# A hybrid decoder step on one core: block sums of the compressed cache taken on VectorE instead of in the accumulating gathers

## The reference, cut to what matters

```python
def block_means(rows):
    B, L = rows.shape[:2]
    nc = L // CMP_BLOCK                       # CMP_BLOCK = 32
    blk = rows[:, :nc * CMP_BLOCK].astype(jnp.float32).reshape((B, nc, CMP_BLOCK) + rows.shape[2:])
    return blk.mean(axis=2).astype(rows.dtype)

past_c = pool_c[page_table].reshape(B, PAST_LEN, 2, NSA_KV_HEADS, NSA_HD)
kc = jnp.concatenate([block_means(past_c).astype(kvc.dtype), block_means(kvc)], axis=1)
```

## Time and profile before

| | before |
|---|---|
| three runs, us | 2081.39, 2088.65, 2123.76 (median 2088.65) |
| the profiled execution's time, us | 2088.65 |
| its span, us | 2086.9 |
| mean granted TensorE clock | 0.931 |
| moved by DMA | 248.81 MB, mean 119 GB/s |

### The profile page before, as it was taken

How to read it: one execution, slowest core, us unless ns; L and a number is a source line. 1 busy time by engine, 2 the same in 40 slices (tenths; PEclk the granted TensorE clock), 3 DMA queues, 4 the chain that set the end, 5 groups by cost and what they waited for, 6 DMA issues and landing times.

```text
span 2086.9 us, 25824 instructions
## 1 busy us (share of the span) xinstructions
PE 1906.2 (91%) x9819; PEld 1313.0 (63%) x9819; DVE 639.6 (31%) x1498; ACT 588.6 (28%) x1251; POOL 425.2 (20%) x514
## 2 busy tenths in 40 slices
PE   4997895899988999997799998999799999999996
PEld 3886674677867765554466666774377777763332
DVE  3232232225000135543546561121233333330002
ACT  2232221222101135563465653003411111110103
POOL 2344234332000111113666630000000000000000
PEclk8998987998998759999999999999899999999998
DMA  7899979982631100002687877211322222211111
GB/s 180 194 214 234 210 180 216 228 196 88 195 85 48 33 10 1 1 1 66 201 278 254 274 227 226 81 61 61 86 61 61 61 78 64 61 61 51 61 38 45
DMA packets 201013, 248.81 MB, mean 119 GB/s; under 512 B 32201, under 2 KB 173850, under 8 KB 192538
## 3 DMA queue, kind: packets, MB, share of 16 engines
q1 hardware_dynamic: 176684, 134.16, 22.0%
q0 software_dynamic: 21248, 109.46, 21.5%
q10 hardware_dynamic: 2960, 3.54, 0.5%
HBM read 236.09 MB, written 19.29 MB: 122 GB/s over the span
## 4 chain that ended last, share of the span: by engine, by line
PE 58%; issue 17%; DMA 13%; DVE 4%; POOL 3%; ACT 3%; SPq 1%; ACTq 1%; POOLq 0%; DVEq 0%
DMA mem<-in_cache_cmp_kv,pidx 12%; PE ps L1505 11%; PE ps L1952 9%; PE ps L1516 5%; PE ps L1739 5%; PE ps L1897 3%; PE ps L1848 3%; PE ps L1826 3%; PE ps L1803 3%; PE ps L1537 2%; PE ps L1722 2%; PE ps L1751 2%; PE ps L1834 1%; PE ps L1587 1%; PE ps L1741 1%
## 5 line engine op out<-in xcount | busy, mean ns | idle before, releaser
L1505 PE MATMUL ps<-mem 128*128 128x288 f32 x1536 | 396.0, 421 | 1.6 <-DVE mem L1380 0.8
L1505 PEld LDWEIGHTS ps<-mem 128*128 128x128 f32 x1536 | 302.7, 198 | 87.6 <-DVE mem L1084 1.0
L1927 PE MATMUL ps<-mem 128*128 128x288 f32 x1408 | 349.4, 410 | 0.0
L1927 PEld LDWEIGHTS ps<-mem 128*128 128x128 f32 x1408 | 267.6, 191 | 72.5
L678 POOL DMA_INDIRECT mem<-in_cache_sel_kv,sidx x192 | 184.0, 958 | 294.1 <-PE ps L1686 194.3
L1952 PE MATMUL ps<-mem 128*128 128x512 f32 (+1 forms) x440 | 203.6, 608 | 0.0
L1952 PEld LDWEIGHTS ps<-mem 128*128 128x128 f32 (+1 forms) x440 | 72.0, 179 | 130.9 <-issue 130.8
L641 POOL DMA_INDIRECT mem<-in_cache_cmp_kv,pidx x56 | 90.2, 1610 | 238.1 <-DMA mem<-in_cache_cmp_kv,pidx 235.7
L708 POOL COPY mem<-mem 128x2 f32<-128x2 f32 x44 | 11.6, 264 | 610.6 <-ACT mem L994 610.6
L1739 PE MATMUL ps<-mem 64*128 64x128 f32 (+3 forms) x256 | 115.4, 537 | 2.1 <-ACT mem L876 2.1
L1516 PE MATMUL ps<-mem 128*128 128x256 f32 (+1 forms) x480 | 107.8, 385 | 0.0
(11 more groups left out here) (300 smaller groups left out, 2292.1 us busy)
## 6 DMA issues: line engine op xcount, KB each, us to landing
mem<-in_cache_sel_kv SPq DMA_DIRECT2D x320, 128.0 KB, 4.4
mem<-in_w_up SPq DMA_DIRECT2D x44, 512.0 KB, 5.1
mem<-in_w_in SPq DMA_DIRECT2D x32, 512.0 KB, 10.2
mem<-in_w_in SPq DMA_DIRECT2D x14, 1024.0 KB, 5.0
mem<-in_w_down SPq DMA_DIRECT2D x10, 1024.0 KB, 4.9
mem<-in_state_win_kv SPq DMA_DIRECT2D x16, 512.0 KB
out<-in_state_win_kv POOLq DMA_DIRECT2D x8, 1008.0 KB, 16.0
mem<-in_x_prompt SPq DMA_DIRECT2D x8, 512.0 KB, 6.5
```

The source lines that it names most:

```text
L1505: mm = t.matmul(ps[:, 2 * (u % 2) + a, 0:NHF], lhs(k), hT[:, k, a * NHF:(a + 1) * NHF], start=(k == 0), stop=(k == KD - 1))
L1927: mm = t.matmul(ps[:, 2 * (u % 2) + a, 0:NHF], lhs(k), hT[:, k, a * NHF:(a + 1) * NHF], start=(k == 0), stop=(k == KD - 1))
```

## The change

All 64 gathers become plain ones. They take the three slots of `cring` in turn (k % 3 for gather k), and a gather waits only until the slot's former content has been added up (`cg_used` of k - 2). DVE takes each slot with a `tensor_reduce` over its four positions (a view `p c r`: 512 results, groups of four numbers that lie 512 numbers apart), into `cmt[:, b, :]` for q = 0 and into the new buffer `cpart` for q = 1 to 7, and then adds `cpart` to `cmt`. These `rowsum` steps stand at three places of every iteration h < 8: two ahead of `states(h - 1)`, three between `prep2(h)` and `kq(h)`, three behind `kq(h)`. POOL issues three gathers before everything else, eight in head 0, and four and four at the two places of each later head. The old `block_sums` is gone.

```diff
@@ -169,6 +169,7 @@
 
         CROW = 4 * 2 * KV
         cring = [view(CROW, a_kvt + i * CROW) for i in range(3)]
+        cpart = view(2 * KV)
 
         at[0] = a_r
         qb, gb, eb, rb, fb, xb = [[view(N) for _ in range(2)] for _ in range(6)]
@@ -482,7 +483,6 @@
             bb, cc = divmod(kq - NVR, NPC + 1)
             return NC * bb + cc + 1
         NCST = 30
-        CG_STEP = 4
 
         WSEQ = [("wo", 0)] + [x for i in range(1, TT) for x in (("wo", i), ("tr", i - 1))] + [("tr", TT - 1)]
 
@@ -623,26 +623,20 @@
             assert done[0] == NCST, done[0]
 
             pool.wait_ge(idx_ok, 1)
-            ticks = [0]
+            gathers = [0]
 
             def gather(n):
                 for _ in range(n):
-                    k = ticks[0]
-                    for b in range(SB):
-                        q = k - CG_STEP * b
-                        if not 0 <= q < 8:
-                            continue
-                        if q == 0:
-                            wait(pool, cg_used, b - 2)
-                            pool.indirect_dma_start(cring[b % 3], None, cache_rows,
-                                                    bass.IndirectOffsetOnAxis(pidx[:, b, 0:1], 0)).then_inc(cg_in[b % 3], 16)
-                        else:
-                            pool.wait_ge(cg_in[b % 3], 16 * (8 * (b // 3) + q))
-                            pool.indirect_dma_start(cring[b % 3], None, cache_rows,
-                                                    bass.IndirectOffsetOnAxis(pidx[:, b, q:q + 1], 0),
-                                                    compute_op=ALU.add).then_inc(cg_in[b % 3], 16)
-                    ticks[0] += 1
-
+                    k = gathers[0]
+                    if k == SB * 8:
+                        return
+                    wait(pool, cg_used, k - 2)
+                    b, q = divmod(k, 8)
+                    pool.indirect_dma_start(cring[k % 3], None, cache_rows,
+                                            bass.IndirectOffsetOnAxis(pidx[:, b, q:q + 1], 0)).then_inc(cg_in[k % 3], 16)
+                    gathers[0] += 1
+
+            gather(3)
             for h in range(HH + 1):
                 if h < HH:
 
@@ -661,12 +655,12 @@
                     g.tensor_tensor(vms[0:S], vo[0:S, PT, :].unsqueeze(1).to_broadcast([S, SB, P]),
                                     cmask_s[:, :].unsqueeze(2).to_broadcast([S, SB, P]), ALU.mult).then_inc(vm_ok, 1)
                     if h < HH:
-                        gather(2)
+                        gather(4)
                     pool.wait_ge(st_ok, 5 * h)
                     pool.dma_start(hgo_p[0, 0, o, :, :], st[:, NCH, :]).then_inc(hgo_out, 16)
                     pool.dma_start(hgo_s[0, :, o, :, :].rearrange("b k v -> k b v"), s1s).then_inc(hgo_out, 16)
                 if h < HH:
-                    gather(5 - 2 * (h > 0))
+                    gather(8 - 4 * (h > 0))
             for b in range(SB):
                 pool.dma_start(win_s[0, b, 0:WIN - ST].rearrange("w h g d -> w (h g d)"),
                                win_kv[0, b, ST:WIN].rearrange("w h g d -> w (h g d)")).then_inc(win_out, 16)
@@ -810,7 +804,7 @@
                 if new:
                     h_sig(h, 0, qb)
                 else:
-                    act.wait_ge(cg_used, SB)
+                    act.wait_ge(cg_used, SB * 8)
                     kv_rows(U_KV)
                 if old:
                     h_ktok(h - 1)
@@ -1092,12 +1086,23 @@
             mark(v.memset(att, 0.0))
             mark(v.memset(att_s, 0.0))
 
-            def block_sums(b):
-
-                r = cring[b % 3]
-                dve.wait_ge(cg_in[b % 3], 16 * 8 * (b // 3 + 1))
-                link(v.tensor_tensor(r[:, 0:4 * KV], r[:, 0:4 * KV], r[:, 4 * KV:8 * KV], ALU.add))
-                v.tensor_tensor(cmt[:, b, :], r[:, 0:2 * KV], r[:, 2 * KV:4 * KV], ALU.add).then_inc(cg_used, 1)
+            sums = [0]
+
+            def rowsum(n):
+
+                for _ in range(n):
+                    k = sums[0]
+                    if k == SB * 8:
+                        return
+                    b, q = divmod(k, 8)
+                    dve.wait_ge(cg_in[k % 3], 16 * (k // 3 + 1))
+                    out = cmt[:, b, :] if q == 0 else cpart
+                    ins = v.tensor_reduce(out, cring[k % 3].rearrange("p (r c) -> p c r", r=4), AX.X, ALU.add)
+                    ins.then_inc(cg_used, 1)
+                    dve.wait_ge(cg_used, k + 1)
+                    if q:
+                        link(v.tensor_tensor(cmt[:, b, :], cmt[:, b, :], cpart, ALU.add))
+                    sums[0] += 1
 
             def prep2(h):
 
@@ -1170,22 +1175,21 @@
 
             for h in range(HH + 1):
                 new, old = h < HH, h > 0
-                if not new:
-                    block_sums(SB - 1)
                 if old:
                     silu(h - 1, 3, gb, 2 * h)
                 if new:
                     silu(h, 0, qb, 2 * h + 1)
                 if old:
                     masked(h - 1)
+                if new:
+                    rowsum(2)
                 if old:
                     states(h - 1)
                 if new:
                     prep2(h)
+                    rowsum(3)
                     kq(h)
-                for b in range(SB):
-                    if new and (CG_STEP * b + 7) // 5 + 1 == h:
-                        block_sums(b)
+                    rowsum(3)
                 if old:
                     head_out(h - 1)
```

## The result

| | kernel before | changed kernel |
|---|---|---|
| median of four runs beside each other | 2085.02 us (2080.42 to 2123.76) | 2156.22 us (2155.26 to 2161.16) |
| ratio | 1 | 1.0358, 95% interval 1.0335 to 1.0382 |

A forecast was written before the change was run, and what follows sets the result against it. PE's stalls for POOL's masked values, queued behind serial gathers, were taken as the bound; new DVE sums make the heads 8.8 + 7 x 61.3 = 437.9 us instead of 415.7, so 2088.65 + 22 = 2111 us, range 2025 to 2165.

The forecast's parts named there:

- The stalls at L658 go: Recurrence heads: all 52.5 us of PE's waits for POOL's masked values vanish; at most 73.4 us gained.
- DMA at the plain rate isn't the limit: Head stage: plain gathers move 295 GB/s, so a head's 11.6 MB take 39 us and supply does not limit.
- The reduce at 3.63 us: DVE row sums: a 2048-element reduce with jumps costs 1.70 ns an element plus 154 ns, as L1044 did.
- slower rival: DVE reduce: jumps of 2048 bytes cost twice the unit price, 4.41 us; 67.5 us a head, 2159 us total; chance 0.30.
- fast rival: DVE reduce: jumps are free, 2.28 us; loop 50.2 us a head, 2025 us total; chance 0.20.
- 61.3 us a head and 8.8 for the first: Head loop: 58.3 us with six sums before head_out plus 3.0 for PE's clock; first head waits 8.8 for a bank.
- the paragraph on new waits: Head stage: POOL waits for slot sums, delaying state stores, loads and masked values; costed at nothing.
- Behind the last head nothing changes: All stages after the recurrence heads keep their former time; no cost added.

The follow-up runs named there:

- nosum: Changed kernel with the row sums left out (eight-element copies in place of the reduces, means missing): 2110.53 us, ratio to before 0.9918.
- cont: Changed kernel with the reduce over four adjacent elements instead of strided ones (sums the wrong quadruples): 2038.77 us, ratio to before 0.9583.
- again2: Changed kernel unaltered, rerun and profiled on a further chip: 2157.86 us, ratio to before 1.0325; the profiled run took 2160.7 us.
- again: Changed kernel unaltered, for a second profile: 2163.02 and 2164.29 us in two runs, 2209.65 and 2214.01 in two; lower groups' ratio to before 1.0168.
- again3: Changed kernel unaltered, on a last chip; with again4 fourteen runs: eight at 2164.95 to 2178.72 us, six at 2203.32 to 2221.66.
- again4: Changed kernel unaltered once more, same chip as again3; with it fourteen runs: eight at 2164.95 to 2178.72 us, six at 2203.32 to 2221.66.
- fill_before: Kernel before with four dummy matmuls ahead of each of the prompt attention's first 64 units: 2137.87 to 2166.03 us, ratio to before 1.0277.

## Why the prediction was off, step by step

- **The stalls at L658 go.** Right: none is left among PE's waits.
- **DMA at the plain rate isn't the limit.** Right. Landings fell from 10.7 to 6.2 us, and nosum runs at 49.7 us a head with all the gathers in place, at 238 GB/s. (In the changed kernel itself the rate over 104 to 480 us is 190, below before's 210, since POOL waits 336.6 us for DVE.)
- **The reduce at 3.63 us.** It measured 3.68. L1044, the one small reduce with jumps, gave 1.70 ns an element; the new one has (3684 - 154) / 2048 = 1.72. Jumps of 2048 bytes cost what jumps of 32 do: the slower rival's doubled price has no ground here. The fast rival's 2.28 us is what cont measured with the jumps taken out. The Trainium skill's page "SBUF — State Buffer" (section "Door 1: The DMA port swizzle") has a penalty for each access that enters a new 16-byte line. These runs agree with it, 1.40 us for 2048 elements; none of them has a jump inside a line, which would test it. The skill's page "VectorE: DVE Perf Modes" (section "The perf-mode tier table") has tensor_reduce at 1x in every column, and its table has no column for jumps: adjacent elements ran at 1.04 ns each, those 2048 bytes apart at 1.72.
- **61.3 us a head and 8.8 for the first.** again2 starts its keys at 77.07, 147.19, 207.48, 268.35, 329.51, 390.79, 452.15 and 519.68. The first interval (70.1) has the wait of 9.1 in it, 61.0 without; the next five are 60.3 to 61.4. The last is 67.5, and this was not foreseen: one DVE instruction takes 7.08 us there instead of 0.82, with POOL's masked values running beside it (last section). The sum is 442.6 us, where 437.9 were forecast and before had 415.7: +27 instead of +22. Without those 6.3 us it would be 436.3. So the one step of the head stage that failed is in the paragraph on new waits, which cost POOL's masked values at nothing: it asked what PE pays when they come late, and not what DVE pays when they run beside it.
- **"Behind the last head nothing changes".** This is the step that failed. The prediction took every later stage from one profiled execution as if it were fixed, and with it the 72 us at half clock at the start of the prompt attention. That length is drawn anew in each execution. In the comparison that was measured it fell short on three of before's four runs and long on all four of the changed kernel's, which put 36 us on top of the change's own cost. The two runs beside the profiled one, 2081 and 2124, had it in plain sight: 42 us between runs of one kernel were a stage with more than one length, not scatter.
- **What the change costs, like against like.** Means of the groups of runs, us:

| chip of | stretch | before (runs) | changed kernel (runs) | difference |
|---|---|---|---|---|
| first comparison | long | 2123.8 (1) | 2157.2 (4) | 33 |
| again | short | 2128.0 (3) | 2163.7 (2) | 36 |
| again | long | 2161.5 (4) | 2211.8 (2) | 50 |
| again2 | long | 2123.9 (8) | 2158.1 (6) | 34 |
| again3, again4 | short | 2125.1 (1) | 2170.8 (8) | 46 |
| again3, again4 | long | 2171.2 (16) | 2212.1 (6) | 41 |

By stages it is 27 us from first to last keys. By the first scores of the prompt attention it is 30 to 35 us between profiles of one chip (746.7 of again2 against 715.1 of fill_before, which is before up to there; 747.0 and 747.8 against 713.3 on the last chip). What is left up to 50 us I can't place: the long stretches come in more than one length (271 and 284 us of the stage), and the sample attention came out between 6 us shorter (again4, 366.6 against 372.2) and 8 longer (again, 372.1 against 364.5) than in a profile of before on the same chip.

Of the 71 us, then, some 35 are the change's and some 36 the draw's. The direction of the forecast was right and so was its mechanism in the head stage; its own size was 22 for some 35, and of the 49 us between forecast and measurement 36 come from what it left out. That 2156.22 us lies inside the stated range of 2025 to 2165 is luck: the upper end was set by a reduce of 4.41 us, and the reduce took 3.68.

The better version comes from the same reading. The gain on gathers is real, and the price was the stride: with two adds over adjacent halves in place of the strided reduce, the sums take 2.6 us instead of 4.4 and nearly fit DVE's idle time. That kernel is 0.974 to 0.981 of before, like against like on two chips, and some 86 us under the changed one on the last chip (2079 to 2093 against 2165 to 2179).

## What to carry to other kernels

Before a forecast is made against one profiled execution, look at its granted clock stage by stage and at the distance of its runs: a stage at 0.50 in the profile and runs that lie 40 us apart say that the baseline has more than one length, and a difference must be taken like against like. When DMA work is moved to DVE, work out the order of DVE's queue up to the instruction that PE waits for, and price a reduce by its stride: here it was cheaper to add halves twice than to reduce over jumps once. Look as well at what POOL runs beside the new instructions of DVE: those here that read two tensors from SBUF stood still until POOL was done. An engine that had slack hides such a wait; when the slack is used up, it reappears on the path.
